# DMA transposes for query/key units, mixed branches and the residual of the gated feed-forward in a two-layer block

## The reference

```python
h = rmsnorm(x, g_mix)
proj = h @ w_in                          # 2048 -> 3*2048 (q, k, v) + 3*2048 (gates)
q, k, v = ...                            # 16 heads of 128 each
gates = sigmoid(proj[..., 3*2048:])      # three gates of width 2048
o_a = stick_breaking_attention(q[:, :4], k[:, :4], v[:, :4])
qn, kn = rmsnorm(q[:, 4:], q_gain), rmsnorm(k[:, 4:], k_gain)
o_b = moba_attention(...)                # heads 4 to 9
o_c = dilated_attention(...)             # heads 10 to 15
merged = (gates[0] * (flat(o_a) @ w_branch[:512])
          + gates[1] * (flat(o_b) @ w_branch[512:1280])
          + gates[2] * (flat(o_c) @ w_branch[1280:]))
x = x + merged @ w_out
h2 = rmsnorm(x, g_ffn)
gu = h2 @ w_gu                           # 2048 -> 2*5632
x = x + (silu(gu[..., :5632]) * gu[..., 5632:]) @ w_down
```

## Time and profile before

| | us |
|---|---|
| median of three runs | 2511.6 |
| lowest and highest | 2510.41, 2512.24 |
| the profiled execution | 2510.78 |
| its span from first to last instruction | 2508.7 |
| busy in it: PE / DVE / ACT / POOL | 2482.3 / 1455.7 / 1362.6 / 67.2 |

### The profile page before, as it was taken

One profiled execution on the slowest core, in us unless ns is written; L12 is line 12 of the kernel. 1 busy time (PEld: TensorE's weight loads), 2 busy tenths in 40 slices (PEclk: granted clock), 3 DMA queues, 4 the chain that ended last, 5 costly groups with the idle time before them and its releaser, 6 DMA issues.

```text
span 2508.7 us, 29869 instructions
## 1 busy us (share of the span) xinstructions
PE 2482.3 (99%) x11102; PEld 2059.0 (82%) x11102; DVE 1455.7 (58%) x1550; ACT 1362.6 (54%) x1721; POOL 67.2 (3%) x78
## 2 busy tenths in 40 slices
PE   8999999999999999899999999999999999999999
PEld 7888878888888888788888888888888888888887
DVE  5888566556455465656566645555555545555554
ACT  6887566455455465544565544444555444544553
POOL 0110000000000000011100000000000000000000
PEclk9999999999999999999999999999999999999999
DMA  8997657677677676465655566665577666766665
GB/s 276 266 267 203 203 184 219 212 221 215 194 216 210 193 215 204 137 200 184 196 172 166 178 193 190 189 193 183 189 206 207 204 193 201 208 204 193 201 193 168
DMA packets 305142, 504.56 MB, mean 201 GB/s; under 512 B 70432, under 2 KB 70744, under 8 KB 304760
## 3 DMA queue, kind: packets, MB, share of 16 engines
q1 hardware_dynamic: 300184, 485.88, 64.1%
q0 software_dynamic: 4688, 16.93, 3.0%
q10 hardware_dynamic: 144, 0.01, 0.0%
HBM read 476.52 MB, written 4.47 MB: 192 GB/s over the span
## 4 chain that ended last, share of the span: by engine, by line
PE 98%; ACT 1%; DVE 0%; issue 0%; DMA 0%; POOL 0%; ACTq 0%; DVEq 0%
PE acc L425 32%; PE acc L427 32%; PE acc L426 32%; PE tp L442 1%; PE po L600 0%; PE sc L570 0%; ACT w_hi L681 0%; ACT yb L848 0%; DMA raw<-w_in_dram 0%; PE tp L588 0%; DVE w_lo L1076 0%; PE po L602 0%; ACT ev L688 0%; ACT junk L731 0%; DVE h L1340 0%
## 5 line engine op out<-in xcount | busy, mean ns | idle before, releaser
L1076 DVE TENSOR_TENSOR w_lo<-raw,w_hi 128x1024 fp32r<-128x1024 f32 x888 | 1078.0, 1224 | 893.1 <-ACT w_hi L681 892.6
L681 ACT ACTIVATE w_hi<-raw 128x1024 fp32r<-128x1024 f32 x888 | 932.2, 1059 | 958.1 <-PE acc L427 931.4
L425 PE MATMUL acc<-w_lo,a_hi 128*128 128x512 f32 x2304 | 902.4, 392 | 8.8 <-DVE a_lo L1133 8.1
L427 PE MATMUL acc<-w_hi,a_lo 128*128 128x512 f32 x2304 | 897.6, 390 | 0.0
L426 PE MATMUL acc<-w_hi,a_hi 128*128 128x512 f32 x2304 | 897.4, 389 | 0.0
L425 PEld LDWEIGHTS acc<-w_lo,a_hi 128*128 128x128 f32 x2304 | 433.5, 188 | 98.3 <-DVE a_lo L1133 8.1
L427 PEld LDWEIGHTS acc<-w_hi,a_lo 128*128 128x128 f32 x2304 | 433.2, 188 | 90.8
L426 PEld LDWEIGHTS acc<-w_hi,a_hi 128*128 128x128 f32 x2304 | 433.6, 188 | 88.5
L425 PE MATMUL acc<-w_lo,b_hi 128*128 128x512 f32 x1120 | 436.2, 389 | 0.3 <-DVE w_lo L1076 0.3
L427 PE MATMUL acc<-w_hi,b_lo 128*128 128x512 f32 x1120 | 435.8, 389 | 0.0
L426 PE MATMUL acc<-w_hi,b_hi 128*128 128x512 f32 x1120 | 435.7, 389 | 0.0
(11 more groups left out here) (167 smaller groups left out, 916.4 us busy)
## 6 DMA issues: line engine op xcount, KB each, us to landing
raw<-w_in_dram SPq DMA_DIRECT2D x272, 512.0 KB, 4.2
raw<-w_down_dram SPq DMA_DIRECT2D x216, 512.0 KB, 4.2
raw<-w_gu_dram SPq DMA_DIRECT2D x176, 512.0 KB, 4.2
raw<-w_up_dram SPq DMA_DIRECT2D x128, 512.0 KB, 3.9
raw<-w_out_dram SPq DMA_DIRECT2D x64, 512.0 KB, 4.1
raw<-w_branch_dram SPq DMA_DIRECT2D x32, 512.0 KB, 3.7
tap_sum<-tap_add POOLq DMA_DIRECT2D x20, 512.0 KB, 7.1
skew_dram<-line_dram POOLq DMA_DIRECT2D x12, 192.0 KB, 4.3
```

Of the source, the lines that this page charges most:

```text
L425: nc.tensor.matmul(out, xh, wl, start=s == 0 and k == 0, stop=False)
L427: mm = nc.tensor.matmul(out, xl, wh, start=False, stop=s == n - 1 and k == KS - 1)
L681: nc.scalar.activation(w_hi[:, ring], raw[:, ring], ACT.Copy).then_inc(hi_ready, 1)
L1076: nc.vector.tensor_tensor(w_lo[:, ring], raw[:, ring], w_hi[:, ring].bitcast(F32), ALU.subtract).then_inc(lo_ready, 1)
```

## The change

Of the seventeen PE turns of the second layer behind its first norm, sixteen are replaced by the way over planes: 8 in query/key, 4 of the branches' sums, 4 of the chunks of h. Three sets of buffers stand for the one of before ("ff", "qk", "mix"). The DMA transposes of a query/key unit n are issued ahead of the load of slot 3 of unit n+2, and joined on ACT in unit n+1 behind the rounding of slot 0 of unit n+2. Those of a branch sum are issued ahead of the load of slot 1 of the second unit after, and joined in the first unit after behind the rounding of its slot 6. Those of a chunk of h are issued at the start of the loads of the second unit after and joined like those of a branch. The function that rounds is now apart from the one that joins. The waits on `turned` become waits on `planes_ready`, the loops of SP in these stages and that of ACT in query/key become written out, as do ACT's and DVE's over the feed-forward's blocks; DVE's query/key loop and ACT's and DVE's branch loops stay. The mean of squares before the gated feed-forward moves behind its first unit, and the zeroing of wide on GpSimd behind the square root.

The diff, cut to its core:

```diff
-T_IN, T_N1, T_N2, T_QK, T_ATT, T_M, T_N3, T_FF = 0, 12, 20, 28, 44, 60, 68, 76
+T_IN, T_N1, T_N2, T_ATT, T_FF = 0, 12, 20, 28, 44
...
-X_MLP, X_FF = 0, 16
+X_MLP, X_QK, X_M, X_N3, X_FF = 0, 16, 24, 28, 32
...
-        planes = at("planes", 144, [P, TT, 2, W], U16)
-        planesT = at("planesT", 148, [P, 2, 4, S], U16)
-        joined = at("joined", 152, [P, 4, S])
+        planes, planesT, joined = {}, {}, {}
+        for stage, kb in (("ff", 144), ("qk", 176), ("mix", 112)):
+            planes[stage] = at(f"planes_{stage}", kb, [P, TT, 2, W], U16)
+            planesT[stage] = at(f"planesT_{stage}", kb + 4, [P, 2, 4, S], U16)
+            joined[stage] = at(f"joined_{stage}", kb + 8, [P, 4, S])
...
-            with sp.Fori(0, 3 * NCH) as j:
-                src = w_in2[:, :, bass.ds(sp.snap(j * W), W)]
+            for v in range(3 * NCH):
                 for s in range(SPU):
-                    load(s, G_QK + j * SPU + s, src[:, ks(s)])
+                    if s == 3 and 2 <= v < 2 * NCH + 2:
+                        turn_planes(X_QK + v - 2, "qk")
+                    load(s, G_QK + v * SPU + s, w_in2[:, ks(s), v * W:(v + 1) * W])
...
-            with sp.Fori(1, NCH) as j:
+            for j in range(1, NCH):
...
                 for b in range(3):
...
                     for s in range(SPU):
-                        load(s, g + (b * SPU + s), src[:, ks(s)])
...
+                        if (b, s) == (1, 1):
+                            turn_planes(X_M + j - 1, "mix")
+                        c0 = (3 + b) * D + j * W
+                        load(s, g + (b * SPU + s), w_in2[:, ks(s), c0:c0 + W])
...
+            for j in range(NCH):
                 for s in range(SPU):
-                    load(s, G_OUT2 + j * SPU + s, src[:, ks(s)])
+                    if (j, s) == (1, 1):
+                        turn_planes(X_M + 3, "mix")
+                    if j > 1 and s == 0:
+                        turn_planes(X_N3 + j - 2, "mix")
+                    load(s, G_OUT2 + j * SPU + s, w_out2[:, ks(s), j * W:(j + 1) * W])
...
                 for v in range(3 * NCH):
+                    if b == 0 and v < 2:
+                        turn_planes(X_N3 + 2 + v, "mix")
...
-                    turn(zz, (z_ready, i * 2 + (21 + p_)), (took, i * 4 + (K_QK + 2 * p_ - 1)))
...
-                    slots(g + b * SPU, u + b, 0, 2, a_hi, a_lo, pair=b % 2)
-                    if b == 0:
-                        turn(zz, (z_ready, j + 28), (split_lo, S_M - 3 + j * 2))
-                    slots(g + b * SPU, u + b, 2, SPU, a_hi, a_lo, pair=b % 2)
+                    slots(g + b * SPU, u + b, 0, SPU, a_hi, a_lo, pair=b % 2)
...
-                slots(G_OUT2 + j * SPU, U_OUT2 + j, 0, 2, m_hi, m_lo, split0=split0, pair=j % 2)
-                if j == 0:
-                    turn(zz, (z_ready, 32), (split_lo, S_M + 5))
-                else:
-                    turn(h[:, :, j - 1, :], (h_ready, 2 * NCH + j), (split_lo, S_N3 + 2 * j - 3))
-                slots(G_OUT2 + j * SPU, U_OUT2 + j, 2, SPU, m_hi, m_lo, split0=split0, pair=j % 2)
+                slots(G_OUT2 + j * SPU, U_OUT2 + j, 0, SPU, m_hi, m_lo, split0=split0, pair=j % 2)
...
-            def join_planes(n, lo_done, dst, k0):
+            def join_planes(n, stage, free):
                 act.wait_ge(planes_turned, 32 * (n + 1))
-                act.wait_ge(split_lo, lo_done)
...
+            def round_joined(n, stage, dst, k0, gain0=None):
                 for q in range(2):
                     act.wait_ge(join_done, 2 * n + q + 1)
-                    nc.scalar.activation(dst[:, k0 + 2 * q:k0 + 2 * q + 2, :],
-                                         joined[:, 2 * q:2 * q + 2, :], ACT.Copy
-                                         ).then_inc(split_hi, 1)
+                    if gain0 is None:
+                        nc.scalar.activation(dst[:, bass.ds(k0 + 2 * q, 2), :],
+                                             joined[stage][:, 2 * q:2 * q + 2, :], ACT.Copy
+                                             ).then_inc(split_hi, 1)
+                        continue
+                    for k in (2 * q, 2 * q + 1):
+                        a_ = nc.scalar.activation(dst[:, k0 + k, :], joined[stage][:, k, :],
+                                                  ACT.Copy,
+                                                  scale=cols[:, gain0 + k0 + k:gain0 + k0 + k + 1])
+                    a_.then_inc(split_hi, 1)
...
-            with act.Fori(0, NCH) as i:
-                for p_ in range(2):
...
-                    for q in range(2):
-                        act.wait_ge(turned, T_QK + 2 * p_ + q + 1 + i * 4)
-                        for k in range(2):
-                            head = i * 8 + (4 * p_ + 2 * q + k)
-                            a_ = nc.scalar.activation(
-                                qkT[:, bass.ds(head, 1), :].rearrange("p k s -> p (k s)"),
-                                tp[:, q, k * S:(k + 1) * S], ACT.Copy, scale=qkg[:, bass.ds(head, 1)])
-                        a_.then_inc(took, 1)
+            def turn_heads(v):
+                join_planes(X_QK + v, "qk", (took, K_QK + 2 * v))
+                for q in range(2):
+                    act.wait_ge(join_done, 2 * (X_QK + v) + q + 1)
+                    for k in range(2):
+                        head = 4 * v + 2 * q + k
+                        a_ = nc.scalar.activation(qkT[:, head, :], joined["qk"][:, 2 * q + k, :],
+                                                  ACT.Copy, scale=qkg[:, head:head + 1])
+                    a_.then_inc(took, 1)
+            for v in range(2 * NCH):
+                g = G_QK + v * SPU
+                ticks(g, SPU, SPU + 1)
+                if v:
+                    turn_heads(v - 1)
+                ticks(g, SPU + 1, SPU + RING)
+                act.wait_ge(rs_ok, 5)
+                act.wait_ge(z_ready, 20 + v)
+                evacuate(v % 2, g + SPU, ev[:, v % 2], 4)
+                ticks(g, SPU + RING, 2 * SPU)
             def attend(n):
...
+                    if (u, s) == (U_V, RING):
+                        turn_heads(2 * NCH - 1)
...
-                    ticks(g, RING + b * SPU, RING + b * SPU + 2)
+                    ticks(g, RING + b * SPU, RING + b * SPU + 3)
                     if b == 0:
-                        split(T_M - 2 + j * 2, m_hi, j * 4 - 4)
-                    ticks(g, RING + b * SPU + 2, RING + (b + 1) * SPU)
+                        join_planes(X_M - 1 + j, "mix", (split_lo, S_M - 2 + j * 2))
+                        round_joined(X_M - 1 + j, "mix", m_hi, j * 4 - 4)
+                    ticks(g, RING + b * SPU + 3, RING + (b + 1) * SPU)
                     act.wait_ge(z_ready, j + 28)
                     evacuate(b % 2, g + (b + 1) * SPU, gate[:, b], 4, ACT.Sigmoid)
                 merge(g + 3 * SPU, j * 4, j + 28, 1)
...
+            def turn_mid(c):
+                join_planes(X_N3 + c, "mix", (split_lo, S_M + 8 + 2 * c))
+                round_joined(X_N3 + c, "mix", a_hi, 4 * c, G_FFN2)
+                squares(5, c, h[:, :, c], 64 + 2 * c)
...
-                ticks(g, RING, RING + 2)
+                ticks(g, RING, RING + 3)
                 if j == 0:
-                    split(T_M + 6, m_hi, 12)
-                ticks(g, RING + 2, RING + SPU)
+                    join_planes(X_M + 3, "mix", (split_lo, S_M + 6))
+                    round_joined(X_M + 3, "mix", m_hi, 12)
+                else:
+                    turn_mid(j - 1)
+                ticks(g, RING + 3, RING + SPU)
...
                 evacuate(j % 2, g + SPU, ev[:, j % 2])
-                split(T_N3 + 2 * j, a_hi, 4 * j, G_FFN2)
-                squares(5, j, h[:, :, j], 64 + 2 * j)
...
+                    if b == 0 and j == 0:
+                        turn_mid(3)
...
-            def part_planes(n, z):
-                dve.wait_ge(z_ready, z)
+            def part_planes(stage, src, ready):
+                dve.wait_ge(*ready)
                 for tk in range(TT):
-                    nc.vector.tensor_copy(planes[:, tk], zz[:, tk].bitcast(U16).rearrange(
+                    nc.vector.tensor_copy(planes[stage][:, tk], src[:, tk].bitcast(U16).rearrange(
                         "p (c t) -> p t c", t=2)).then_inc(planes_ready, 1)
...
-                    dve.wait_ge(turned, T_QK + 2 * p_ + i * 4)
+                    dve.wait_ge(planes_ready, i * 4 + (2 * X_QK + 2 * p_))
...
                                             ).then_inc(z_ready, 1)
+                    part_planes("qk", zz, (z_ready, i * 2 + (21 + p_)))
                     ticks(g, SPU + RING + 1, 2 * SPU)
...
+                part_planes("mix", zz, (z_ready, j + 29))
...
-                    ticks(g, RING + b * SPU, RING + b * SPU + 2)
+                    ticks(g, RING + b * SPU, RING + b * SPU + 3)
                     if b == 0:
-                        split(S_M - 2 + j * 2, m_hi, m_lo, j * 4 - 4)
-                    ticks(g, RING + b * SPU + 2, RING + (b + 1) * SPU)
```

(73 more changed lines are left out.)

45 lines of the change are left out of this document (19 added, 26 removed).

## The result

The changed kernel takes 2532.93 us (median of six runs, 2531.53 to 2534.45), the kernel before 2511.03 beside it: a ratio of 1.0086 (95% interval 1.0077 to 1.0096), 21.9 us slower. I had forecast 2517, with a range up to 2529. The direction was right, the size was four times too small, and the time lies 4 us outside the range.

A forecast was written before the change was run, and what follows sets the result against it. TensorE was taken as the bound, busy 99% of the span. Query/key +12.7, branches -3.7+0.6 and residual -4.4 made +5.2 on 2510.78, thus 2516.0; adding 0.8 for the median, 2517 us, range 2502 to 2529.

The forecast's parts named there:

- the value of the turns: PE transposes removed: a turn worth 0.92 us, 16 of them 14.7 us, of which 7.4 us in query/key.
- The chain in query/key: Query/key: each evacuation waits on the previous one through copies, transposes and joins; 24.5 us a unit, costing +12.7 us.
- e+8.3: Query/key, e being the start of ACT's evacuation of a unit: scaled zz ends and DVE's copies follow 8.3 us later.
- the landing of a pair: Query/key: time from first issue of two DMA transposes until ACT can join, 4.5 to 6.5 us, taken as 5.5.
- 8L-183.3: Query/key cost in us for a loop of L us: +12.7 at 24.5, +4.7 at 23.5, +20.7 at 25.5.
- -3.7+0.6-4.4: Branches save 3.7 us and lose 0.6 at the first output unit; the residual saves 4.4.
- T+9.2: Branches, T being when PE finishes a unit: ACT is ready to join from here; transposes land at T+13.1.
- The cover of 0.1 us: Branches: w_lo of slot 7 ready at T+18.9, wanted at T+19.0; 1 us stall if DMA takes 1 us longer.
- (1): Rival, query/key: the cover holds, L under 21.8, 15.4 us gained, 2496 us; chance 0.12.
- (3): Rival: landing over 6 us beside two loads, plus 1 us in each mixed place; 2521 to 2530 us, chance 0.18.
- the four mixed places: Three places in the branches and the first output unit, where rival (3) adds 1 us each.
- (4): Rival, clock: query/key waits lower the granted clock seven times, 2.6 us each, 18 in all; 2535 us, chance 0.04.

The follow-up runs named there:

- alone: The changed kernel with query/key turned on PE as before, so only branches and residual go over planes: 2505.22 us, ratio 0.9975, 6.3 us below the kernel before.
- the kernel with slot 1 and the earlier branches: Changed kernel with query/key transposes ahead of the load of slot 1 instead of 3, branches' transposes ahead of slot 0 instead of 1: 2495.74 us, ratio 0.9938.
- slot 1: The changed kernel with only the query/key transposes moved ahead of the load of slot 1 instead of slot 3: 2497.76 us, ratio 0.9945.

## Why the prediction was right or wrong

**The bound, and the value of the turns: right.** PE lost 128 instructions, and where all else is hidden the eight turns of query/key are worth 7.5 us measured, 7.4 forecast. (The rows give 22.69-21.76 = 0.93 us for a turn where the forecast writes 0.92; nothing hangs on it.)

**The chain in query/key: right in every link but one.** The forecast had copies at e+8.3, transposes at e+12.3, the joins standing still for 2 to 4 us (5.3 in the period shown, 4.0 to 8.9 over the stage), PE waiting 2.7 us in a unit (16.6 in seven, so 2.4), and the loop closed. The step that failed is the landing of a pair. I took 5.5 us, from two pairs of the feed-forward that took 5.4 and 6.0, and gave the loads just ahead almost no weight; the period shown has 6.5 and one pair has 8.5. A microsecond of landing is 8 us of time, because the loop runs eight times. The stage cost 25.4 us where 12.7 was forecast. The eight pairs together took 11.3 us more than eight times 5.5, and the four scaled copies took 1.59 us instead of 1.44, eight times over 1.2 us: 12.5 of the 12.7. (The forecast's own formula, 8L-183.3, gives 23.9 us with the measured L of 25.9; it lacks the 1.4 us by which the last pair, behind the last period, is slower than the one shown.) So the mechanism held and the size was off by the landing. The same error made the range too narrow: its upper end took the single transposes' 3.2 to 5.2 us as a bound, but the two pairs that ScalarE had waited for stood 1.5 us behind the last load, not right behind one, and a single transpose now took up to 7.0 us.

The spans differ by 21.2 us where 5.2 was forecast. The 3.3 us that the stage leaves over are small terms: 1.0 ahead of it, which the change isn't shown to cause; 1.5 in the attention, from the clock behind PE's last wait, which the sum had at nothing; and 0.8 less saved behind.

**Branches and residual: nearly right.** Forecast -3.7+0.6-4.4 = -7.5; alone they gave -6.3. The join of a branch waits 3.9 us for the DMA, from T+9.2 to T+13.1 as worked out, and the first output unit's wait is 0.5 us for 0.6 forecast. Two joins of the residual did wait, 1.2 and 0.2 us, where none was forecast, without a wait of PE. The cover of 0.1 us was too thin to be called covered.

**The rivals.** (1), all hidden, gives 2496: that is what the kernel with slot 1 and the earlier branches does, at 2495.7. It was the right price for another order. (3), a longer landing, was the case that came, beyond its own upper end of 2530; the extra microsecond that it had in the four mixed places did not come. (4), the clock: it does fall, to 0.96 in the stage, but not at the price of 18 us: where ScalarE's joins set the pace it gives no time back when raised, and its one measured cost is the 1.5 us at the first attention step. The page on the clock gate ("TensorE: Matmul & The Clock Gate", Part 1, of the Trainium skill) has idleness halve the clock. The trace agrees: the granted clock is 0.50 from 1170 to 1176 us, right behind PE's wait of 5.2 us. The 261 GB/s of the Trainium skill's "DMA: Bandwidth & Descriptors", section "Latency and other measured facts", would have had me go lower still; no pair that ScalarE waited for took less than 4.5 us here, and the slowest took 8.8.

## What to carry to other kernels

Before work is moved to an asynchronous queue, write down for one period everything that the queued instruction stands behind, in its own queue and through the waits of what is ahead of it, and follow the result back to the start: if the circle takes longer than the bounding engine's period, every period pays the difference. Here one line's position in SyncE's list was worth 35 us, with the same work on every engine. A latency that enters such a circle has to be taken from transfers in the same neighbourhood, not from the same operation elsewhere, and its error counts once for each turn of the loop.

## What the runs showed of the hardware

A DMA transpose of 128x1024 16-bit elements from SBUF to SBUF landed 3.2 us (median) after its issue when SyncE had issued no load in the 3 us before (slot 1), and 5.6 us when a 512 KB load stood right ahead of it (the change); SyncE was held 2.6 us for a pair in the first case and 3.9 to 5.8 in the second. Moving only that load behind the pair brought the median back to 4.0 us. A lower granted clock, 0.96 over 230 us, cost nothing that could be seen where another chain set the pace. Where PE set it, right behind a wait of 3.2 to 6.6 us, the same fall cost 1.4 to 2.6 us, and matmuls that nobody reads, put into the wait, took that away.
